# A rebuilt router, first gather and tail, with 60 matrix products that nobody reads

## The reference

```python
z = x @ w_in                                  # 2048 x 9216
y_a = s5_mixer(...); y_b = hgrn2_mixer(...)   # two recurrences
merged = sigmoid(gate_a) * (y_a @ w_ba) + sigmoid(gate_b) * (y_b @ w_bb)
h = layer_norm(ALPHA * x + merged @ w_o, ln1_g, ln1_b)
# router: the best of 4 groups, then the best 2 of its 8 experts
grp = top_k(softmax(h @ w_gr + b_gr), 1);  exp = top_k((h @ w_er + b_er)[grp], 2)
moe = sum over the 2 experts of weight * (silu(h @ w_g[e]) * (h @ w_u[e])) @ w_d[e]
ple = sigmoid(h @ w_pg) * (p @ w_pp)
x_new = layer_norm(ALPHA * h + moe + ple, ln2_g, ln2_b)
```

## Time and profile before

| | us |
|---|---|
| median of 3 runs | 1623.52 |
| lowest, highest | 1616.81, 1628.93 |
| the profiled execution's own time | 1617.29 |
| its span, first to last instruction | 1615.5 |

### The profile page before, as it was taken

How to read it: one execution, slowest core, us unless ns; L and a number is a source line. 1 busy time by engine, 2 the same in 40 slices (tenths; PEclk the granted TensorE clock), 3 DMA queues, 4 the chain that set the end, 5 groups by cost and what they waited for, 6 DMA issues and landing times.

```text
span 1615.5 us, 21195 instructions
## 1 busy us (share of the span) xinstructions
PE 1435.6 (89%) x8725; PEld 1082.9 (67%) x8725; DVE 758.8 (47%) x1499; ACT 333.8 (21%) x468; POOL 96.9 (6%) x94
## 2 busy tenths in 40 slices
PE   6969999999999999998999989888999698789671
PEld 4968998777788678768999975563465265346220
DVE  3749777888864246315565554302213142120237
ACT  3413331000010010015344442131202101200102
POOL 2730000000010100000010020000000000000002
PEclk9979999999999799979999996799999899999976
DMA  8424444333333433424554470389999999999991
GB/s 220 151 92 164 142 148 133 109 109 109 108 121 118 130 100 110 136 98 137 180 188 169 170 295 27 137 337 359 392 405 409 409 403 372 409 406 405 409 380 55
DMA packets 139039, 353.23 MB, mean 219 GB/s; under 512 B 20644, under 2 KB 21724, under 8 KB 138416
## 3 DMA queue, kind: packets, MB, share of 16 engines
q1 hardware_dynamic: 135944, 341.99, 57.8%
q0 software_dynamic: 2992, 9.81, 2.1%
HBM read 344.60 MB, written 7.18 MB: 218 GB/s over the span
## 4 chain that ended last, share of the span: by engine, by line
PE 75%; DMA 12%; DVE 7%; issue 2%; ACT 2%; SPq 1%; DVEq 0%; ACTq 0%
PE bank L520 72%; DMA mslot<-in_w_exp_up 6%; DMA mslot<-in_w_exp_down 5%; DVE lo L1574 1%; DVE atok L2327 1%; ACT hi L1303 1%; PE bank L535 1%; PE bank L792 1%; DMA stS<-in_state_hgrn 1%; SPq L1158 1%; DMA ident<-in_consts 1%; ACT htok L1422 0%; DVE stS L1896 0%; DVE stats L2408 0%; PE bank L907 0%
## 5 line engine op out<-in xcount | busy, mean ns | idle before, releaser
L520 PE MATMUL bank<-XT,raw 128*128 128x264 f32 x1280 | 309.1, 402 | 0.0
L520 PEld LDWEIGHTS bank<-XT,raw 128*128 128x128 f32 x1280 | 250.3, 198 | 47.3 <-issue 3.2
L1574 DVE TENSOR_TENSOR lo<-raw,hi 128x2048 fp32r<-128x2048 f32 x68 | 157.3, 2314 | 132.7 <-ACT hi L1303 132.6
L520 PE MATMUL bank<-mslot,Xg 128*32 128x512 f32 (+1 forms) x1024 | 146.6, 664 | 41.1 <-DMA mslot<-in_w_exp_up 40.0
L1303 ACT ACTIVATE hi<-raw 128x2048 fp32r<-128x2048 f32 x68 | 130.1, 1914 | 233.3 <-PE bank L520 229.8
L520 PE MATMUL bank<-XH,hi 128*128 128x264 f32 x512 | 148.9, 291 | 7.4 <-DVE lo L1574 6.2
L520 PE MATMUL bank<-XL,hi 128*128 128x264 f32 x512 | 147.3, 288 | 0.0
L520 PE MATMUL bank<-XH,lo 128*128 128x264 f32 x512 | 146.3, 286 | 0.0
L520 PEld LDWEIGHTS bank<-mslot,Xg 128*32 128x32 f32 (+1 forms) x1024 | 40.6, 123 | 124.5 <-issue 123.6
L520 PE MATMUL bank<-HT,mslot 128*128 128x264 f32 x512 | 116.3, 387 | 0.0
L520 PE MATMUL bank<-mslot,hidT 128*32 128x512 f32 (+1 forms) x512 | 79.6, 719 | 33.2 <-DMA mslot<-in_w_exp_down 33.2
(11 more groups left out here) (389 smaller groups left out, 2268.4 us busy)
## 6 DMA issues: line engine op xcount, KB each, us to landing
raw<-in_w_in SPq DMA_DIRECT2D x72, 1024.0 KB, 5.1
mslot<-in_w_exp_gate SPq DMA_DIRECT2D x128, 512.0 KB, 11.2
mslot<-in_w_exp_up SPq DMA_DIRECT2D x128, 512.0 KB, 12.8
mslot<-in_w_exp_down SPq DMA_DIRECT2D x64, 1024.0 KB, 14.0
raw<-in_w_out SPq DMA_DIRECT2D x16, 1024.0 KB, 5.0
mslot<-in_w_ple_gate SPq DMA_DIRECT2D x16, 1024.0 KB, 14.3
raw<-in_w_branch_b SPq DMA_DIRECT2D x8, 1024.0 KB, 5.0
raw<-in_w_branch_a SPq DMA_DIRECT2D x8, 1024.0 KB, 5.0
```

The source lines that it names most:

```text
L520: return nc.tensor.matmul(out, w, x, start=start, stop=stop)
L1574: v.tensor_tensor(lo[:, n % RD, :], raw[:, n % RD, :], hi[:, s % RH, :].bitcast(F32), ALU.subtract).then_inc(lo_done, 1)
```

## The change

It rebuilds four places.

1. **Router.** `raw_logits` multiplies the un-normalized `XT` with router weights that DVE has scaled with the gain beforehand (`w_gained`), four products after each block of `w_out`. The layer norm is applied afterwards to the 36 logits of each token. `h_features` and `logits` are gone, and DVE no longer normalizes `htok`. `HT` is made later, in step 0 and 1, from `XT` (`spread_scalars`, `features`). The router's weights are loaded with feature k*128+p on partition p, in runs of 16 and 128 bytes.
2. **First gather.** Step 0 gathers with f32 products from `htok` directly, in three portions between the parts of `gate_up`; `hH`, `hL`, `hS` are made behind it. In place of the two ple chunks PE has `keep_clock`: 60 products of 264 columns of the tile `MH` into bank 0, which nobody reads.
3. **Steps.** The two steps with two experts move from 1 and 2 to 5 and 6. The ple blocks are at steps 2, 3, 4 and 7, `rest` is at step 8.
4. **Tail.** The last `down` loads come in three pieces, statistics are taken block by block between the last scatters, `ln2` is loaded as 8 rows and spread by 8 products, gain and bias are applied in two fused passes over halves of 1024 columns, five stores go out, and the flag is read after them.

```diff
+FILLERS = 60
...
-PLANS = [[list(range(FIXED))] + PAIRS[2:4] + QUADS] + [PAIRS] * 4
+PLANS = [[list(range(FIXED))] + QUADS[:4] + PAIRS[2:4] + QUADS[4:]] + [PAIRS] * 4
...
-PLE_AT = {0: 0, 3: 1, 5: 2, 7: 3}
-PLE_AHEAD = (0, 1)
-REST_AT = 5
+PLE_AT = {2: 0, 3: 1, 4: 2, 7: 3}
+REST_AT = 8
+FIRST_GATHER = {0: (0, 1, 2), 1: (3, 4), 2: (5, 6, 7), 3: ()}
...
+        def pieces(rnd, g):
+
+            return ((0, 2), (2, 3), (3, 4)) if (rnd, g) == (0, len(PLANS[0]) - 1) else ((0, 2), (2, 4))
...
+            def raw_logits(j):
+
+                if j == 0:
+                    pe.wait_ge(w_gained, 1)
+                    b = side("wall")
+                    mm(b[:, 0:72], ones[:, :], wsum[:, :, :].rearrange("p i n -> p (i n)"), True, True).then_inc(
+                        misc_ready, 1)
+                for J in range(4 * j, 4 * j + 4):
+                    last = mm(bank[7][0:36, 0:NT], wrr[:, J], XT[:, J], J == 0, J == KD - 1)
+                if j == 3:
+                    last.then_inc(logT_done, 1)
...
+                    raw_logits(j)
...
-            def h_features(k):
-                b = side(("ht", k))
...
-            def logits(k):
...
+            def keep_clock():
+
+                for i in range(FILLERS):
+                    mm(bank[0][:, 0:NT], MH[:, i % 4, 0:128], MH[:, i % 4, :], True, True)
...
+                if cb == 0 and kq == 0:
+                    pe.wait_ge(ht_done, KD)
...
-            for kq in PLE_AHEAD:
-                ple_gate(0, kq)
+            keep_clock()
...
+            def first_gather(u):
+
+                b = side(("ga", 0, 0, u))
+                if u == 0:
+                    pe.wait_ge(norm_act, 3)
+                    pe.wait_ge(zeroed, 3)
+                    pe.wait_ge(sel_ready, 1)
+                sel = [selm[:, 0, 0, 0:128].bitcast(F32), selm[:, 0, 1, 0:128].bitcast(F32),
+                       sels[0:NB, 0, 0:128].bitcast(F32)]
+                for q in range(2):
+                    ks = slice((2 * u + q) * 128, (2 * u + q + 1) * 128)
+                    for tt, (t0, tn) in enumerate(TOK):
+                        last = mm(b[:, q * 256:q * 256 + 128], htok[0:tn, tt, ks], sel[tt], tt == 0, tt == 2)
+                last.then_inc(misc_ready, 1)
...
+                    if (rnd, g) == (0, 0):
+                        for u in FIRST_GATHER[s]:
+                            first_gather(u)
+                        stored(("ga", 0, 0, 2 * s))
+                        stored(("ga", 0, 0, 2 * s + 1))
...
+            def norm_rows(again):
+
+                pe.wait_ge(ln2_ld, 32)
+                for r in range(8):
+                    b = side(("row", again, r))
+                    mm(b[:, :], ident[0:8, r:r + 1].to_broadcast([8, 128]), ln2row[:, :], True, True).then_inc(
+                        misc_ready, 1)
...
-                gate_up_done(sp, rnd, len(plan) - 1)
-                for i, n in enumerate(("ln2_gain", "ln2_bias")):
-                    sp.dma_start(ln2[:, i, :], t[n].to_broadcast([P, D])).then_inc(ln2_ld, 16)
...
-            for k in HT_ACT:
-                b, read = side(("ht", k))
-                nc.scalar.activation(HT[:, k, :], b[:, 0:NT], ACT.Identity, bias=ln1[:, 1, k:k + 1],
-                                     scale=ln1[:, 0, k:k + 1]).then_inc(read, 1)
...
+            def features():
+
+                for k in range(KD):
+                    if k % 8 == 0:
+                        act.wait_ge(ht_mul, 2 + k // 8 * 2)
+                    nc.scalar.activation(HT[:, k, :], XT[:, k, :], ACT.Identity, bias=lnk[:, 1, k:k + 1],
+                                         scale=lnk[:, 0, k:k + 1]).then_inc(ht_done, 1)
...
+                if n == N_O:
+                    b, read = side("lnk")
+                    dve.wait_ge(r_ld, 64)
+                    v.tensor_copy(lnk[:, :, :].rearrange("p i k -> p (i k)"), b[:, 0:2 * KD]).then_inc(read, 1)
+                    side_read(dve, "lnk")
+                    link(v.tensor_tensor(wrb[:, :, :], wrr[:, :, :],
+                                         lnk[:, 1, :].unsqueeze(2).to_broadcast([P, KD, 36]), ALU.mult))
+                    settle()
+                    link(v.tensor_tensor(wrr[:, :, :], wrr[:, :, :],
+                                         lnk[:, 0, :].unsqueeze(2).to_broadcast([P, KD, 36]), ALU.mult))
+                    link(v.tensor_reduce(wsum[:, 1, :], wrb[:, :, :].rearrange("p k n -> p n k"), AX_X, ALU.add))
+                    settle()
+                    v.tensor_reduce(wsum[:, 0, :], wrr[:, :, :].rearrange("p k n -> p n k"), AX_X,
+                                    ALU.add).then_inc(w_gained, 1)
...
+            def h_lows():
+
+                dve.wait_ge(h_high, 3)
+                dve.wait_ge(misc_ready, misc["ga", 0, 0, 7][0] + 1)
+                v.tensor_tensor(hS[32:32 + NB], by_k(htok[0:NB, 2, :]), hS[0:NB].bitcast(F32),
+                                ALU.subtract).then_inc(split_done, 1)
+                for half in range(2):
+                    for tt in range(2):
+                        h_low(tt, half)
+                dve.wait_ge(split_done, 5)
+
...
+            def last_give_back(g):
+
+                store(0, g, 0)
+                store(0, g, 1)
+                scatter(0, g, 0)
+                scatter(0, g, 1)
+                side_read(dve, ("sc", 0, g, 0, 2))
+                side_read(dve, ("sc", 0, g, 0, 1))
+                side_read(dve, ("sc", 0, g, 0, 0))
...
+                for tt, (t0, tn) in enumerate(TOK[0:2 + again]):
+                    for step in range(2):
+                        for half in range(2):
+                            cs = slice(1024 * half, 1024 * (half + 1))
+                            if step == 0:
+                                v.scalar_tensor_tensor(out=ynorm[0:tn, tt, cs], in0=atok[0:tn, tt, cs],
+                                                       scalar=mv[0:tn, tt, 0:1], in1=ln2[0:tn, 0, cs],
+                                                       op0=ALU.subtract, op1=ALU.mult).then_inc(gained, 1)
+                            else:
+                                dve.wait_ge(gained, 4 * again + 2 * tt + half + 1)
+                                v.scalar_tensor_tensor(out=ynorm[0:tn, tt, cs], in0=ynorm[0:tn, tt, cs],
+                                                       scalar=rstd[0:tn, tt:tt + 1], in1=ln2[0:tn, 1, cs],
+                                                       op0=ALU.mult, op1=ALU.add).then_inc(f_out, 1)
+
...
-            final_statistics(0)
-            final_scalars(0)
-            final_statistics(1)
-            final_scalars(1)
-            final_statistics(2)
-            final_scalars(2)
-            final_gain_bias(1)
-            final_gain_bias(2)
...
```

372 lines of the change are left out of this document (216 added, 156 removed).

## The result

The changed kernel takes **1605.8 us** in the median of 7 runs (1602.7 to 1607.3), against 1623.5 of the kernel before in the same comparison: ratio 0.9895, 95% interval [0.9876, 0.9915]. That is a gain, but of 1% only: 18 us saved, where the forecast had 68 on the profiled execution (1617.3 less 1549.0; the recorded 69 comes from rounded parts). So the forecast of 1549 and its range up to 1578 are wrong. The profiled execution took 1604.5, of which 1602.6 is the span; against the profiled one of before (1617.3) it saves only 12.8 us. Single executions of over 1800 us, which came now and then and with the kernel before too, are in no median or ratio here.

A forecast was written before the change was run, and what follows sets the result against it. TensorE was taken to bound the dense part, the weight stream the expert part. Restart at 993.7, 512 + 15 us of stream (landing 1520.7), a 26.5 us tail and 1.8 around the span made 1549; range 1528 to 1578.

The forecast's parts named there:

- Dense part: Blocks of `w_out`: four f32 logit products each, 2.0 us a block, make this part longer by 3.8 us.
- Router: From layer norm scalars to first selection: selection at 975.5 against 1013.3, 37.8 us earlier.
- the rival at 1645: Router's weights in 4,096 short runs: DVE and TensorE wait, dense part stops; 143 us of loads, 96 lost; chance 3%.
- a selection after 985: Router: a first selection later than 985, forecast at 975.5, would show the prediction wrong.
- First gather: Step 0: three portions at 1.2 GHz in 9.0 us, first part 5.4; stream restarts at 993.7, 42.8 us earlier.
- The stream: Expert weights: 200 MiB at 409.5 GB/s in 512 us plus 15 lost; last landing at 1520.7.
- the 30 us in sum: Weight stream: holes of over 30 us in sum would show the prediction wrong.
- The new order of the steps: Weight stream: four-expert steps without ple first remove old holes, 20 us before; new holes of 12 us taken.
- The tail: From last weights' landing to span's end: 26.5 us, between 22 and 30, against 45.65 before; 19 us saved.
- TensorE as the bound of steps 2 to 4: Rival at 1567: the ring of ten cannot cushion a 33 us ple block, each step loses 6 us more; chance 18%.

The follow-up runs named there:

- e_again: The changed kernel run once more, unchanged; 1605.3 us, ratio 0.9892 to the kernel before.
- e_ple_odd: Against the changed kernel, ple blocks in steps 1, 3, 5 and 7 instead of 2, 3, 4 and 7; 1604.2 us, ratio 0.9872.
- e_ple_1347: Against the changed kernel, ple blocks in steps 1, 3, 4 and 7, so only that of step 2 moved; 1595.5 us, ratio 0.9825.
- e_between: Against the changed kernel, scatters of step 8's blocks 0 and 1 right behind the first piece of its down products; 1597.1 us, ratio 0.9836.
- e_small_dve: Against the changed kernel, the 8 sample tokens' final gain and bias by two fused VectorE passes, not ACT and POOL; 1598.7 us, ratio 0.9849.
- e_tail2: Against the changed kernel: two down pieces, step 8's block 0 and 1 scatters between, gain and bias by broadcasting loads, sample tokens on VectorE; 1586.1 us, ratio 0.9782.
- e_best2: e_tail2 with ple blocks in steps 1, 3, 4 and 7 and 16 more unread products behind the counting; 1571.6 us, ratio 0.9691.
- e_fill_gather: Against the changed kernel, 16 more unread products behind the counting, ahead of the first gather; 1601.3 us, ratio 0.9862.

## Why the prediction was wrong, step by step

On the profiled executions the forecast missed by 1604.5 - 1549 = 55.5 us. It splits so:

- **Dense part, +3.8: right**, a block's eight records took 1.97 for 2.0. The scalars of e_again, 967.9, are 3.9 behind those of before, 964.0, at the same granted clock in the two stretches in which the change's own profile differs. In the profiled execution of the change 7.0 us more came, most of them from the clock in older code. The page of before was a good draw too: 6 us under its median, which I noted and left in the range.
- **Router: right.** Forecast 11.4 us from the scalars to the selection, measured 11.3. The router's weights, in their short runs, landed in 6.3 and 6.6 us, where the rival at 1645 needed over 115; it did not come:

```profile
wrr<-in_w_expert_router POOLq DMA_DIRECT2D x1, 256.0 KB, 6.3
```
The 60 products outlast VectorE's choice by 0.8, forecast 1. One sign of being wrong that the prediction named did show, a selection after 985: it was made at 985.2 to 986.1. But that is the 7 us of the clock in older code; in e_again the gather behind it starts at 979.2.
- **First gather: right in its clock, 2.2 us too cheap.** Half a portion took 1.87 at 0.50, so 0.62 a product and not 0.5 by columns; step 0's first part 6.0 for 5.4. The first slot came at 1003.45 for 993.7: 7.0 + 2.8. A part of the 2.8 is the clock's draw again: from the scalars to the first slot it took 28.6 us here and 27.5 in e_again.
- **The stream, forecast at 512 + 15 us: the first step that failed.** From the first slot to the last landing it took 552.2, so 40.2 were lost where I had 15. This is over the 30 us in sum that the prediction named as a sign of being wrong. The window from 1530 on shows 17 of them: 3.7 MB in 26 us, the third piece's loads waiting for slots behind `norm_rows`. The prediction put this at nothing: I had moved the piece's size into the tail and never asked which slots its loads would take. Another 17 are dents, nearly all while TensorE is busy throughout: 6.8 MB short of 405 GB/s from 1020 to 1500. I had 12 and priced steps by the sum of a step's work. e_ple_odd and e_ple_1347 show that it also matters which step a ple block stands in; how the work lies within a step was not tested. The rest is 3 for the first landing and the difference between 405 and 409.5 GB/s. The new order of the steps, from which I expected 8 us, shows no gain: from the first slot to the turn the kernel before took 518.1 us with 5.1 us of loads less, the change 522.5 and e_again 526.0.
- **The tail, forecast 26.5, measured 46.9: the second step that failed.** I gave VectorE the statistics of blocks 0 and 1 before the landing, but TensorE's queue has both scatters behind the last piece: from the landing to the end of statistics it took 21.3 us (to 1577.0) for 9.1. And I let POOL's passes run beside VectorE's: VectorE's eight took 18.1 for 9.2. Both could be read beforehand. `norm_rows`, pieces and scatters stand in that order in `expert_round`. And in the trace of the kernel before, VectorE's `nmr`, one number a row, takes 0.15 us once and 3.47 the next time, beside POOL's pass of 1593.05:

```profile
1590.60 0.15 DVE L2420 SCALAR_TENSOR_TENSOR nmr<-mv,rstd 8x1 f32<-8x1 f32 x1
1594.09 3.47 DVE L2420 SCALAR_TENSOR_TENSOR nmr<-mv,rstd 128x1 f32<-128x1 f32 x1
1600.89 1.25 DVE L2420 SCALAR_TENSOR_TENSOR nmr<-mv,rstd 128x1 f32<-128x1 f32 x1
```
The second ends with POOL's first pass (1597.5) and the third with its second (1602.1). In between, four instructions of VectorE's statistics, which have one input, take 2.46 us beside POOL's second pass and 2.45 without any.

Between turn and end e_between gives back 8.8 us and e_small_dve 6.0 (4.6 of them by its edit); e_tail2, which mends the slots too, gives back 22.
- **The rivals.** TensorE as the bound of steps 2 to 4, forecast 18%, is the one that the dents bear out: those at 1150 and 1290 make 5.3 MB, 13 us. But the forecast itself had 12 us of holes, so little of the rival's 18 came on top. No rival had the end of the stream or the tail as its place, and each of these was larger.

With slots, POOL and order mended, ple moved and the clock held in the first gather, e_best2 is at 1571.6 in its profile too. That is inside the range, but still 23 us above the forecast, and it needed edits that the forecast did not have.

## What to carry to other kernels

When a last transfer is cut into smaller pieces, number the slots of the ring again, and see whose use frees the last ones. Follow each in-order queue from the last landing to the end, and place nothing "in the wait" that stands ahead of what ends the wait. Work on an idle engine is not free if it stops the engine that is the path: POOL's two passes over 8 rows cost VectorE 8.5 us. And compare marks with the same kernel run again: here the clock alone moved one by 7 us.

## What the runs showed of the chip

- VectorE's fused pass over 128x1024 with two SBUF operands took 1.27 us (two in a row 2.48), and up to 5.5 while POOL had a two-operand pass over 8x2048 running.
- One f32 product of 128 columns took 0.62 us at the granted clock 0.50 (1.87 for three) and 0.35 at 1.00 (from 978.55 to 984.81 for 18 in e_fill_gather), more than by columns from 264 (0.5 and 0.25).
- The same code was granted 0.69 or 0.85 of the clock between 660 and 680 in different executions; with 0.80 or 0.83 in the 80 us behind it, this is 5.6 of the 7 us by which the scalars moved.
- After a pause of 1.94 us TensorE was granted 0.50 from 990 to 1000. With 16 products in the pause (2.22 us) it was granted 1.00 from 980 to 1000, and 0.50 from 1000 to 1010, though it was busy for all of the 20 us before.
